# The head of an attention layer in another order: rotary key, query latents, key latents

## What is computed

```python
u = rms_norm(x, P['g_pre_mix'][l])
z = jnp.einsum('bsd,de->bse', u, P['w_in'][l])
zq, zkv, zpe, rq, rk, rv, rg, cq, ck, cv, zg = split_cols(z)
q_a = jnp.einsum('bsr,rhd->bshd', rms_norm(zq, P['g_mla_q'][l]), P['w_mla_uq'][l])
q_nope, q_pe = q_a[..., :MLA_NOPE], rope(q_a[..., MLA_NOPE:], pos)
ckv = rms_norm(zkv, P['g_mla_kv'][l])
kpe = rope(zpe[:, :, None, :], pos)[:, :, 0, :]
ckv_all = jnp.concatenate([c_ckv, ckv], axis=1)      # sample only: cached latents first
kv = jnp.einsum('bkr,rhd->bkhd', ckv_all, P['w_mla_ukv'][l])
k_nope, v_a = kv[..., :MLA_NOPE], kv[..., MLA_NOPE:]
```

## Time and profile before

| | |
|---|---|
| three runs | 2769.47, 2771.71, 2781.54 us (median 2771.71) |
| the profiled execution | 2778.73 us, of it the span of the trace 2776.9 us |
| mean granted TensorE clock | 0.962 of full speed |
| busy time | PE 2558.4 us (92%), DVE 1467.9 (53%), ACT 796.3 (29%), POOL 827.0 (30%) |
| chain that ended last | PE 79%, DVE 11%, DVE's sequencer 6% |

### The profile page before, as it was taken

One profiled execution on the slowest core, in us unless ns is written; L12 is line 12 of the kernel. 1 busy time (PEld: TensorE's weight loads), 2 busy tenths in 40 slices (PEclk: granted clock), 3 DMA queues, 4 the chain that ended last, 5 costly groups with the idle time before them and its releaser, 6 DMA issues.

```text
span 2776.9 us, 46587 instructions
## 1 busy us (share of the span) xinstructions
PE 2558.4 (92%) x17836; PEld 2417.4 (87%) x17836; DVE 1467.9 (53%) x2244; ACT 796.3 (29%) x1428; POOL 827.0 (30%) x335
## 2 busy tenths in 40 slices
PE   8889999999989899999788999899999898999996
PEld 7679888988978799999677898798899787999995
DVE  4771564364564845336757516634635647354266
ACT  4342122244334311111224421223433333111112
POOL 3113223222323234333221232132223232333342
PEclk9899999999999999999889999899999999999997
DMA  4112112222222122222121121132222221222222
GB/s 143 39 42 84 54 48 86 66 86 85 80 66 92 49 84 84 84 82 80 60 85 31 57 84 46 40 94 75 82 84 77 65 88 54 79 82 83 83 84 80
DMA packets 65687, 204.73 MB, mean 74 GB/s; under 512 B 7936, under 2 KB 16000, under 8 KB 65360
## 3 DMA queue, kind: packets, MB, share of 16 engines
q10 hardware_dynamic: 47808, 174.08, 20.2%
q1 hardware_dynamic: 17680, 27.90, 3.0%
HBM read 190.93 MB, written 11.03 MB: 73 GB/s over the span
## 4 chain that ended last, share of the span: by engine, by line
PE 79%; DVE 11%; DVEq 6%; issue 2%; ACT 1%; DMA 0%; SPq 0%; ACTq 0%
PE job L354 66%; PE outp L402 4%; PE scores L382 3%; DVE rstd L1025 3%; DVEq L1052 2%; PE scores L277 1%; PE turn L392 1%; DVEq L1088 1%; PE job L363 1%; DVE arena L1016 1%; DVE rstd L1033 1%; DVEq L1189 1%; DVE x L1053 1%; DVEq L1031 1%; PE job L547 0%
## 5 line engine op out<-in xcount | busy, mean ns | idle before, releaser
L354 PE MATMUL job<-arena,w_hi 128*128 128x288 f32 (+1 forms) x9984 | 1817.4, 304 | 46.0 <-DVE q L1190 16.7
L354 PEld LDWEIGHTS job<-arena,w_hi 128*128 128x128 f32 x9984 | 1501.4, 192 | 89.0 <-issue 36.3
L647 POOL TENSOR_TENSOR w_lo<-raw,w_hi 128x1024 fp32r<-128x1024 f32 x331 | 826.8, 2498 | 1918.0 <-ACT w_hi L666 1918.0
L354 PE MATMUL job<-arena,w_lo 128*128 128x288 f32 (+1 forms) x4992 | 1090.6, 298 | 0.0
L354 PEld LDWEIGHTS job<-arena,w_lo 128*128 128x128 f32 x4992 | 820.4, 191 | 0.0
L666 ACT ACTIVATE w_hi<-raw 128x1024 fp32r<-128x1024 f32 x331 | 349.6, 1056 | 1079.1 <-PE job L354 910.2
L999 DVE TENSOR_TENSOR tmp<-job,rstd 128x576 f32<-128x576 f32 x70 | 52.9, 756 | 295.6 <-PE job L354 295.3
L402 PEld LDWEIGHTS outp<-probT,v 128*128 128x128 f32 x992 | 129.9, 192 | 65.5 <-ACT probT L759 53.8
L402 PE MATMUL outp<-probT,v 128*128 128x128 f32 x992 | 152.1, 284 | 30.0 <-DVE arena L1096 21.0
L277 PE MATMUL scores<-q,const 128*128 128x288 f32 (+1 forms) x296 | 100.8, 480 | 69.3 <-ACT q L727 60.2
L988 DVE CAST arena<-tmp 128x576 fp32r<-128x576 f32 x64 | 151.7, 2370 | 4.7
(11 more groups left out here) (152 smaller groups left out, 1763.0 us busy)
## 6 DMA issues: line engine op xcount, KB each, us to landing
raw<-in_w ACTq DMA_DIRECT2D x332, 512.0 KB, 3.5
bias<-in_bias SPq DMA_DIRECT2D x16, 256.0 KB, 2.7
x<-in_x SPq DMA_DIRECT2D x4, 576.0 KB, 8.7
cs<-in_rope SPq DMA_DIRECT2D x4, 576.0 KB, 4.5
out_o_bandk<-k SPq DMA_DIRECT2D x8, 288.0 KB, 3.0
out_o_bandv<-tmp SPq DMA_DIRECT2D x8, 288.0 KB, 3.3
out_y<-x SPq DMA_DIRECT2D x1, 2304.0 KB, 6.9
bias<-in_mem SPq DMA_DIRECT2D x8, 256.0 KB, 3.6
```

Of the source, the lines that this page charges most:

```text
L354: mm = pe.matmul(ps[0:m, po:po + nn], w[:, s, c:c + m], x[:, k, so:so + nn], start=(k == 0 and w is WHI and x is hl[0]), stop=(k == kt - 1 ...
L647: nc.gpsimd.tensor_tensor(WLO[:, u % RING, :], RAWS[:, u % RAW, :], WHI[:, u % RING, :].bitcast(F32), ALU.subtract).then_inc(lo_done, 1)
```

## The change

The order of the six first jobs becomes rotary key, three query latents, two key latents; the weights are laid out in that order. The sums for the first two query blocks are put into the middle of job 3, the one for the third into the middle of job 4 (`amid`), those for the keys behind the job of the cached latents. ACT squares and rounds each block as soon as it is evicted (`latent`). The key latents are rounded before their norm; the reciprocal of the norm (now kept in `rstd2`) is multiplied in when DVE evicts the new keys and values of each head (a product in place of a copy). The cached latents are split by themselves, early. The reciprocal of the queries' norm and the products with cosines and sines leave the first head; the reciprocal of the keys' norm enters it. The normed key latents, which are an output, are made and stored during the second head's `values` step (`store_latents`). The first head's jobs are now cached latents, queries, new latents, values. Both users of `attend_fed` let one more job be unevicted before the first scores.

```diff
@@ -185,7 +185,7 @@
         RTMP = bias_sb[:, 0:NT]
-        rstd_c = TMP[:, 1]
+        rstd_c = rstd2
         MEM_RAW = tiles(bias_sb[:, :], 4)
@@ -333,7 +333,7 @@
                 def project_by_k(s, kt, hl, at_col=0, step=P, m=P, pieces=HALVES, each_ready=0, stats=False,
-                                 each_evicted=False):
+                                 each_evicted=False, amid=None):
@@ -344,6 +344,8 @@
                             stat(k, kt)
+                        if amid and k == kt // 2:
+                            amid()
                         if each_ready and k % each_ready == 0:
@@ -412,6 +414,7 @@
                         pass
+                    values_job = n["job"]
                     groups = {g: pieces(g) for gs in places.values() for g in gs}
@@ -421,7 +424,7 @@
                             fill(j, gap)
-                    evicted(but=begun)
+                    evicted(but=begun + 1)
                     for h, i in flat[:2]:
@@ -432,7 +435,7 @@
                         fill(j, 0)
-                        if j > 1 and (j - 1) % per_group == 0:
+                        if j and (j - 1) % per_group == 0:
                             pe.wait_ge(job_free, l * JOBS + values_job + 2)
@@ -487,29 +490,38 @@
-                for i in range(CR + 1):
-                    project(unit(), KT, U_HL, each_ready=int(i == 0))
-                for k in range(CR):
-                    stat(k, CR)
-                for i in range(QR):
-                    project(unit(), KT, U_HL)
+                def latent_stats(*which):
+
+                    def add():
+                        for k, kt in which:
+                            stat(k, kt)
+                    return add
+
+                project(unit(), KT, U_HL, each_ready=1)
+                for after in (None, None, latent_stats((0, QR), (1, QR)), latent_stats((2, QR)), None):
+                    project(unit(), KT, U_HL, amid=after)
...
+                    s = unit()
+                    past = dict(at_col=QR * P, pieces=[(0, PAST, NT)])
                     if h == 0:
                         wait_ready()
-                    s = unit()
-                    yield from project_by_k(s, CR, CKV_HL, at_col=QR * P)
-                    yield
-                    yield from project_by_k(s, CR, CKV_HL, at_col=QR * P, pieces=[(0, PAST, NT)])
-                    yield
-                    if h == 0:
-                        for k in range(QR):
-                            stat(k, QR)
+                        yield from project_by_k(s, CR, CKV_HL, **past)
+                        for k in range(CR):
+                            stat(k, CR)
                         wait_ready()
-                    yield from project_by_k(s, QR, ZQ_HL)
-                    yield
-                    turn_values(V_TOKENS + [(NT, P, 4), (NT + P, P, 5), (SEQ, P, 6)], but=1)
+                        yield from project_by_k(s, QR, ZQ_HL)
+                        wait_ready()
+                        yield from project_by_k(s, CR, CKV_HL, at_col=QR * P)
+                    else:
+                        yield from project_by_k(s, CR, CKV_HL, at_col=QR * P)
+                        yield
+                        yield from project_by_k(s, CR, CKV_HL, **past)
+                        yield
+                        yield from project_by_k(s, QR, ZQ_HL)
+                        yield
+                    turn_values(V_TOKENS + [(NT, P, 4), (NT + P, P, 5), (SEQ, P, 6)], but=min(h, 1))
@@ -806,23 +818,26 @@
-                for _ in range(CR + 1):
+                def latent(i):
+
+                    act.wait_ge(job_free, l * JOBS + i + 2 + 2)
+                    k, kt = (i, QR) if i < QR else (i - QR, CR)
+                    src, hi_of, name = (ZQ[:, k], ZQ_HL[0][:, k], "mla_q") if i < QR else \
+                        (CKV[:, k, 0:NT], CKV_HL[0][:, k, 0:NT], "mla_kv")
+                    if i == 0:
+                        act.wait_ge(layer_loaded, (l + 1) * 16 * LAYER_LOADS)
+                    square(k, src)
+                    ins = round_hi(hi_of, src, name, k)
+                    if k == kt - 1:
+                        ins.then_inc(rounded, 1)
+                        root_of((rstd2 if i < QR else rstd_c)[:, :], kt * P)
+
+                for i in range(1 + QR + CR):
                     place()
+                    if i >= 2:
+                        latent(i - 2)
                     n["job"] += 1
-                for k in range(CR):
-                    act.wait_ge(job_free, l * JOBS + k + 1 + 2)
-                    square(k, CKV[:, k, 0:NT])
-                root_of(rstd_c, CR * P)
-                for _ in range(QR):
-                    place()
-                    n["job"] += 1
-                evicted()
-                for k in range(QR):
-                    ins = round_hi(ZQ_HL[0][:, k], ZQ[:, k], "mla_q", k)
-                ins.then_inc(rounded, 1)
-                for k in range(QR):
-                    square(k, ZQ[:, k])
-                root_of(rstd2[:, :], QR * P)
+                latent(QR + CR - 1)
@@ -1142,8 +1157,6 @@
-                for k in range(CR):
-                    scale_job(CKV[:, k, 0:NT])
                 scale_job(TMP[:, 0])
@@ -1155,19 +1168,25 @@
                     v.tensor_tensor(K[NOPE:QK, b, 0:NT], TMP[NOPE:QK, 0], RTMP[NOPE:QK, :], ALU.add)
-                invert(rstd_c)
                 scale_job(ZQ[:, 1])
-                for k in range(CR):
-                    v.scalar_tensor_tensor(out=CKV[:, k, 0:NT], in0=CKV[:, k, 0:NT], scalar=g_col("mla_kv", k),
-                                           in1=rstd_c, op0=ALU.mult, op1=ALU.mult)
+                is_ready(split(CKV[:, :, NT:KEYS], CKV_HL[0][:, :, NT:KEYS], CKV_HL[1][:, :, NT:KEYS]))
+                scale_job(ZQ[:, 2])
+                is_ready(lows(lambda k: ZQ[:, k], "mla_q", ZQ_HL, 0, QR))
+                invert(rstd2[:, :])
+                scale_job(CKV[:, 0, 0:NT])
+                v.tensor_tensor(COS[0:QK, :], COS[0:QK, :], rstd2[0:QK, :], ALU.mult)
+                v.tensor_tensor(SIN[QK:P, :], SIN[QK:P, :], rstd2[QK:P, :], ALU.mult)
+                scale_job(CKV[:, 1, 0:NT])
                 dve.drain()
-                z = Z0 + 2 * QR * NT
-                is_ready(split(m_sb[:, QR * NT:QR * NT + CR * KEYS], arena[:, z:z + CR * KEYS],
-                               arena[:, z + CR * KEYS:z + 2 * CR * KEYS]))
-                scale_job(ZQ[:, 2])
-                store()
-                store()
-                is_ready(lows(lambda k: ZQ[:, k], "mla_q", ZQ_HL, 0, QR))
+                is_ready(lows(lambda k: CKV[:, k, 0:NT], "mla_kv", tuple(t[:, :, 0:NT] for t in CKV_HL), 0, CR))
+
+                def store_latents():
+
+                    for k in range(CR):
+                        v.scalar_tensor_tensor(out=CKV[:, k, 0:NT], in0=CKV[:, k, 0:NT], scalar=g_col("mla_kv", k),
+                                               in1=rstd_c[:, :], op0=ALU.mult, op1=ALU.mult)
+                    store()
+                    store()
@@ -1175,13 +1194,10 @@
                         if h == 0:
-                            invert(rstd2[:, :])
-                            v.tensor_tensor(COS[0:QK, :], COS[0:QK, :], rstd2[0:QK, :], ALU.mult)
-                            v.tensor_tensor(SIN[QK:P, :], SIN[QK:P, :], rstd2[QK:P, :], ALU.mult)
-                            for c in range(2):
-                                v.tensor_copy(Q[QK:QK + MASKS, c], COS[QK:QK + MASKS, :])
-                            dve.drain()
+                            invert(rstd_c[:, :])
                         s = job()
+                        if h < 2:
+                            v.tensor_copy(Q[QK:QK + MASKS, b], COS[QK:QK + MASKS, :])
                         v.scalar_tensor_tensor(out=halves(Q[0:QK, b]), in0=job_halves(s, 0, QK), scalar=QK ** -0.5,
@@ -1192,8 +1208,9 @@
                         s = job()
-                        v.tensor_copy(halves(K[0:NOPE, b, 0:NT]), job_halves(s, 0, NOPE))
-                        free(v.tensor_copy(halves(vT[:, 0:NT]), job_halves(s)))
+                        v.tensor_tensor(halves(K[0:NOPE, b, 0:NT]), job_halves(s, 0, NOPE), halves(rstd_c[0:NOPE, :]),
+                                        ALU.mult)
+                        free(v.tensor_tensor(halves(vT[:, 0:NT]), job_halves(s), halves(rstd_c[:, :]), ALU.mult))
@@ -1202,13 +1219,16 @@
                     def values():
+                        if h == 1:
+                            store_latents()
                         s = job()
...
-                    return [new_keys_values, past_keys_values, queries, values]
+                    steps = [new_keys_values, past_keys_values, queries, values]
+                    return [steps[i] for i in (1, 2, 0, 3)] if h == 0 else steps
@@ -1662,12 +1682,12 @@
-        for i in range(CR):
-            add(cols(zkv + i * P))
         pe_w = w[:, zpe:zpe + ROPE]
...
             add(cols(zq + i * P))
+        for i in range(CR):
```

(1 more changed line is left out.)

4 lines of the change are left out of this document (2 added, 2 removed).

## The result

| | before | after |
|---|---|---|
| runs behind the change | 2769.47 to 2781.54, median 2775.24 us (5) | 2737.19 to 2757.76, median 2747.72 us (5) |
| ratio, 95% interval | | 0.9895 [0.987, 0.992] |
| the same kernels again, in two later series | | 0.9924 [0.9904, 0.9945], 0.9929 [0.9905, 0.9952] |
| mean of all executions with a listed clock | 2775.4 us (80 of them, standard error 0.6) | 2752.8 us (17, standard error 1.6) |
| mean granted clock of these | 0.9625 | 0.9676 |

The kernel became faster by 22.6 us in the means, where 12.75 were forecast: a ratio of 0.9954, which lies outside all three intervals. The profiled execution after is the fastest of its five, so its 41.5 us less than the profiled one before is more than the change is worth.

The account below looks back on a forecast made before the run. The prediction took each layer's head to be bound by DVE's serial list, not PE. It summed 6.4 + 6.75 - 2 x 1.1 + 2 x 0.65 + 0.5 = 12.75 us, hence 2758.9 us on the median, range 2751 to 2767.

Parts of the forecast that it names:

- the head: Last projection's end to first maximum in each layer: 19.85 us forecast, saving 6.4 us in the first layer, 6.75 in the second.
- the wait by name and place: Sign, first head: PE's long wait stands before the transposes (L374), ended by the new keys' eviction, at about 6 us.
- no wait at the sums inside jobs 3 and 4: Sign in the latent projections: PE does not wait at the sums; the slower rival, chance 0.04, had it waiting for ACT's squares.
- the reciprocal as DVE's longest piece: Term in the first head: the reciprocal of the keys' norm takes DVE 3.75 us.
- The late work: First head's second mask copy and `store_latents`, now later on DVE: 1.1 us lost in a layer, bounds 0 and 1.95.
- The same `but` in band attention lets the first scores run beside the values' eviction: Band attention: first scores no longer wait for that eviction, saving 0.65 us a layer, bounds 0 and 0.97.
- the same thing in the latent head: First latent head: scores run beside the next head's new keys' eviction instead of behind it, which was a wait of 0.94 us.
- the term for the clock (0.5): First layer behind the long hole: time at the lower clock level becomes as short as in the second; 0.5 us, bounds 0 and 2.3.
- the clock is up: Rival: the shorter hole keeps the clock up, saving 2.25 us more in each layer, 17.3 in all, 2754.4 us; chance 0.14.
- the transposes hold the clock down: Caveat behind the hole: by the skill's rule transposes do not raise the clock, costing 0.75 us a layer; sum 11.3 instead of 12.8.

Follow-up runs that it names:

- x1: The kernel before with only the allowance added (one more job unevicted before the first scores, latent and band attention): mean 2765.7 us, ratio 0.9968 to the kernel before.
- h2: The kernel after without the added allowance in latent and band attention, six executions: ratio 0.9971 to the kernel before.
- w1: The kernel after with late work moved into the first head, whose new keys and values are made before its queries: ratio 0.9925 to the kernel before.
- a1: The kernel after, unchanged, run again: one of two later series, with ratios 0.9924 and 0.9929 to the kernel before.
- a2: The kernel after, unchanged, run once more: one of two later series, with ratios 0.9924 and 0.9929 to the kernel before.
- k1: The kernel after without the reciprocal of the keys' norm (a wait stays in its place): 2758.79 us.
- u1: The kernel after with the query latents' sums behind jobs 3 and 4 instead of in their middle: 2763.34 us in one execution.
- v1: The kernel after with the normed latents, their stores and the second mask copy moved to the first head's values step: ratio 0.9911 to the kernel before.
- b1: The kernel before, unchanged, run once more: ratio 1.0008.

## Why the prediction was wrong

Faster was forecast, by the head, and the head was right: the wait by name and place; 18.64 against 18.75 us; no wait at the sums inside jobs 3 and 4, which PE went through in 2.10 us for eight products and 1.13 for four; and the reciprocal as DVE's longest piece. The late work was mis-sized, 1.8 to 2.3 us for 1.1 in a layer.

The step that failed is "The same `but` in band attention lets the first scores run beside the values' eviction": I took 0.65 us a layer, with bounds of 0 and 0.97, and 0.94 for the same thing in the latent head. Together that is 2 x (0.65 + 0.94) = 3.2 us; measured were 9.7 to 15.2. I priced a removed wait at its own length. In band the removed wait of 0.97 gave only 0.3 us by itself; what it is worth beyond that is clock. The bound of 0.97 should not have been a bound: the earlier trace rows showed a granted clock of 0.71 and 0.82 in the stretches behind the hole, in which such a wait lies, and the term for the clock (0.5) was put on the long hole alone. Of the 22.6 us, 2751.0 x (0.9676 / 0.9625 - 1) = 14.6 go with the clock and (2669.7 - 2662.0) / 0.9625 = 8.0 with the rest. This split gives the clock a little too much, since idle time at the lower level counts in it: in the first layer's long hole, where PE does nothing, 0.68 was granted before (73.6 to 81.8) and 0.81 after (68.7 to 74.4). Without the allowance the change gives 2775.4 - 2768.0 = 7.4 us, or 2765.7 - 2752.8 = 12.9 seen from x1; the other terms of the sum are 12.75 - 3.2 = 9.6, between the two.

The allowance's part can be read off piece by piece. In the latent heads it is 2.3 to 2.6 us in the first layer and 0.3 to 1.8 in the second, from the hole's start to the eleventh maximum; in band 0.3 for the wait and 1.8 to 4.0 for the clock in each layer. Both layers together that is 7 to 13 us. Where the rest of the 15.2 lies stays open: the stretches at the lower level outside these places differ from one execution to the next by several us. That 4 us more are lost with both places undone than with each alone (15.2 against 6.6 + 4.7) is within the errors.

The Trainium skill (TensorE: Matmul & The Clock Gate, Part 1, the section on a second failure mode) tells of short idles between groups of products that let the clock go up and down. h2's 0.99 us with 0.83 against 1.00 agrees. Weighed beforehand, that rule speaks for pricing short waits near a low stretch by the clock.

Of the rivals, "the clock is up" (2754.4 us) came nearest in time, and not for its reason: the clock did fall behind the shorter hole. In w1 it stayed up through the transposes behind 1.64 and 1.81 us, and fell soon after. The first five executions after had luck besides: their mean is 2747.5 us, that of the twelve later ones (a1, a2) 2755.0. Whether the transposes hold the clock down, which the prediction priced at 0.75 us a layer, no run here decides.

## What to carry to other kernels

Where PE waits shortly behind a long stop, count the wait and the products behind it at half speed; removing 1 us there was worth 0.3 to 2.6 us in the first latent head of a layer and some 2 to 4 in band. Such a price is a mean over executions, so take several profiles of either kernel. Read the mean granted clock of every run beside its time: span times clock says roughly whether a difference is work or clock. A single profile can sit some 15 us beside the mean by the pace of its products, so compare several, and before moving DVE work into a gap look at what POOL does in it.

## What the hardware showed

- Back-to-back products of 288 columns with a weight load each ran at 133.3 or 130.0 ns at the full clock, kept over some 380 us, in both kernels. The Trainium skill (TensorE: Matmul & The Clock Gate, Part 2, Back-to-back issue gap) gives a formula for the gap of isolated products, by which 288 columns would take some 122.5 ns (an estimate from it), and for streams with weight loads one pace each at 128 and 512 columns, none at 288. The measurement has two paces at 288, both longer than the estimate.
- DVE's copies and two-operand products in SBUF are held up by POOL's subtraction (2.4 us) beside them: 2.10 instead of 0.46 (k1), 1.51 instead of 0.74 (a1 and u1), 2.78 for two instead of 1.53 (w1 and v1), while the reciprocal was not held up (3.73 in w1, with POOL at work from 66.45 to 68.84). The Trainium skill (SBUF — State Buffer, SBUF: two separate sides) calls the port of the two engines an exclusive lock; these rows agree.
- The same waits do not always cost the same clock. The end of band attention in the first layer, PE's timeline in b1:

```profile
654.12 1.87 PE L402 MATMUL outp<-probT,v 128*128 128x128 f32 x8 [0.69 <-ACT probT L759]
...
657.21 1.65 PE L402 MATMUL outp<-probT,v 128*128 128x128 f32 x6 [0.58 <-ACT probT L759]
```

and in a1, behind the same waits:

```profile
644.33 1.16 PE L404 MATMUL outp<-probT,v 128*128 128x128 f32 x8 [0.69 <-ACT probT L771]
...
646.40 0.94 PE L404 MATMUL outp<-probT,v 128*128 128x128 f32 x6 [0.58 <-ACT probT L771]
```

b1's is one of the five layers counted above.
